# Expert weights split on GpSimd beside the choice of tokens: two low parts leave VectorE's search rounds

## What is computed

```python
def expert_choice_ffn(h, w_router, w_gate, w_up, w_down):
    B, N, D = h.shape
    cap = EC_CAPACITY_FACTOR * N // N_EXPERTS          # 256
    aff = jax.nn.softmax((h @ w_router).astype(jnp.float32), axis=-1)
    g, idx = lax.top_k(jnp.swapaxes(aff, 1, 2), cap)
    xs = jax.vmap(lambda hb, ib: hb[ib])(h, idx)
    hid = jax.nn.silu(jnp.einsum('becd,edf->becf', xs, w_gate)) * jnp.einsum('becd,edf->becf', xs, w_up)
    ys = jnp.einsum('becf,efd->becd', hid, w_down) * g[..., None].astype(h.dtype)
    return jax.vmap(lambda yb, ib: jnp.zeros((N, D), yb.dtype).at[ib.reshape(-1)].add(yb.reshape(-1, D)))(ys, idx)
```

## Time and profile before

| | us |
|---|---|
| median of 3 runs | 3572.96 |
| lowest and highest run | 3571.43, 3576.19 |
| span of the profiled execution | 3570.0 |
| PE busy in that span | 3353.1 (94%) |
| DVE busy | 1936.9 (54%) |
| ACT busy | 1366.7 (38%) |
| POOL busy | 560.6 (16%) |

### The profile page before, as it was taken

How to read it: one execution, slowest core, us unless ns; L and a number is a source line. 1 busy time by engine, 2 the same in 40 slices (tenths; PEclk the granted TensorE clock), 3 DMA queues, 4 the chain that set the end, 5 groups by cost and what they waited for, 6 DMA issues and landing times. The chain is left out here.

```text
span 3570.0 us, 75034 instructions
## 1 busy us (share of the span) xinstructions
PE 3353.1 (94%) x31456; PEld 2882.7 (81%) x31456; DVE 1936.9 (54%) x3309; ACT 1366.7 (38%) x1927; POOL 560.6 (16%) x792
## 2 busy tenths in 40 slices
PE   7999999999799998989999989929999999999997
PEld 5788888787577877878888878829999999999997
DVE  4666667666544655652122146575655565556553
ACT  5445454444256664320000013314444444444442
POOL 3455555555000000000000000000000100010001
PEclk9999999999899999999999999959999999999999
DMA  4221212211234434421111144335666666666662
GB/s 142 55 82 56 84 54 62 82 50 38 82 119 142 142 107 142 135 65 40 48 29 46 48 143 154 135 127 182 205 207 211 200 204 208 211 199 202 210 209 74
DMA packets 361076, 439.96 MB, mean 123 GB/s; under 512 B 15093, under 2 KB 300053, under 8 KB 359957
## 3 DMA queue, kind: packets, MB, share of 16 engines
q1 hardware_dynamic: 351640, 403.19, 34.5%
q0 software_dynamic: 9216, 33.56, 4.0%
HBM read 369.58 MB, written 67.13 MB: 122 GB/s over the span
## 5 line engine op out<-in xcount | busy, mean ns | idle before, releaser
L2620 PE MATMUL bank<-ex_x_hi,ex_w_lo 128*128 128x256 f32 x2048 | 581.7, 284 | 3.6 <-DVE ex_x_lo L2809 3.6
L2621 PE MATMUL bank<-ex_x_lo,ex_w_hi 128*128 128x256 f32 x2048 | 580.4, 283 | 0.0
L2622 PE MATMUL bank<-ex_x_hi,ex_w_hi 128*128 128x256 f32 x2048 | 580.2, 283 | 0.0
L2616 DVE TENSOR_TENSOR ex_w_lo<-ex_w_loaded,ex_w_hi 128x2048 fp32r<-128x2048 f32 x190 | 429.5, 2289 | 239.9 <-ACT ex_w_hi L2612 235.5
L2612 ACT ACTIVATE ex_w_hi<-ex_w_loaded 128x2048 fp32r<-128x2048 f32 x192 | 359.7, 1905 | 226.6 <-PE bank L2622 183.9
L2620 PEld LDWEIGHTS bank<-ex_x_hi,ex_w_lo 128*128 128x128 f32 x2048 | 393.8, 192 | 4.6 <-issue 4.0
L2621 PEld LDWEIGHTS bank<-ex_x_lo,ex_w_hi 128*128 128x128 f32 x2048 | 393.9, 192 | 0.6
L2622 PEld LDWEIGHTS bank<-ex_x_hi,ex_w_hi 128*128 128x128 f32 x2048 | 393.9, 192 | 0.0
L2688 POOL CAST ex_idx<-moe_idx_all 128x2 uint32 (+1 forms) x16 | 3.0, 186 | 1802.2 <-POOLq L79 1487.0
L264 PE MATMUL bank<-columns_columns_hi,weights_weights_lo 128*128 128x512 f32 x544 | 226.8, 417 | 9.4 <-DVE columns_columns_lo L848 4.4
L266 PE MATMUL bank<-columns_columns_hi,weights_weights_hi 128*128 128x512 f32 x544 | 214.1, 394 | 0.0
(11 more groups left out here) (458 smaller groups left out, 8266.0 us busy)
## 6 DMA issues: line engine op xcount, KB each, us to landing
ex_w_loaded<-in_wg SPq DMA_DIRECT2D x64, 1024.0 KB, 5.4
ex_w_loaded<-in_wu SPq DMA_DIRECT2D x64, 1024.0 KB, 6.4
ex_w_loaded<-in_wd SPq DMA_DIRECT2D x64, 1024.0 KB, 5.1
plain_weights<-in_w_in SPq DMA_DIRECT2D x70, 512.0 KB, 4.6
gl_ada_tile<-in_ada_w SPq DMA_DIRECT2D x48, 512.0 KB, 4.2
plain_columns<-hT_dram SPq DMA_DIRECT2D x14, 1024.0 KB, 7.4
sc_w_loaded<-in_sc_w_in SPq DMA_DIRECT2D x23, 512.0 KB, 6.5
plain_columns<-in_x SPq DMA_DIRECT2D x16, 512.0 KB, 5.8
```

Source lines behind the costliest of these rows:

```text
L2616: nc.vector.tensor_tensor(w_lo[c % SPLIT][:], raw[:, c % LOADED, :], w_hi[c % SPLIT][:].bitcast(F32), ALU.subtract).then_inc(s["lo"], 1)
L2620: nc.tensor.matmul(psum, ll, rh, start=first, stop=False)
L2621: nc.tensor.matmul(psum, lh, rl, start=False, stop=False)
L2622: return nc.tensor.matmul(psum, lh, rh, start=False, stop=last)
```

## The change

GpSimd gets a body in the block of `choose`: it waits for the high part of chunk 0 and subtracts it from the loaded chunk in one instruction of 128 x 2048, then the same for chunk 1, and counts up `lo` after each. VectorE's twelve pieces are taken out of the rounds, with their waits.

```diff
@@ choose
             def _(act):
                 beside.scalar(act)
 
+            @block.gpsimd
+            def _(pool):
+                beside.pool(pool)
+
             @block.vector
             def _(dve):
                 go = Line(dve, s["chain_v"])
@@ choose, search
                         parts(n + r)
-                        beside.vector(dve, n + r)
                         go.settle()
                         dve.wait_ge(s["summed"], n + r + 1)
@@ experts, class Beside
-            def vector(self, dve, r):
-
-
-                c, piece = divmod(r - 3, 6)
-                if 0 <= c < 2:
-                    of = slice(piece * 352, min(piece * 352 + 352, W))
-                    if piece == 0:
-                        dve.wait_ge(s["hi"], c + 1)
-                    ins = nc.vector.tensor_tensor(w_lo[c][:, of], raw[:, c, of], w_hi[c][:, of].bitcast(F32), ALU.subtract)
-                    if piece == 5:
-                        ins.then_inc(s["lo"], 1)
+            def pool(self, pool):
+
+                for c in range(2):
+                    pool.wait_ge(s["hi"], c + 1)
+                    nc.gpsimd.tensor_tensor(w_lo[c][:], raw[:, c, :], w_hi[c][:].bitcast(F32), ALU.subtract).then_inc(s["lo"], 1)
```

## The result

The changed kernel takes 3579.01 us (median of 20 runs, 3575.13 to 3583.78) against 3573.02 (20 runs, 3569.34 to 3576.19). The ratio is 1.0018, with a 95% interval of 1.0012 to 1.0025. It is slower by 6 us. The median lies inside the bound of 0.2%, the upper end of the interval beyond it.

The account below looks back on a forecast made before the run. The kernel was taken as TensorE-bound where it has work, the changed stretch as bound by a VectorE chain. Stalls of 3.1 + 3.2 less a gain of 1.1 give 5.2 us lost: 3572.96 + 5.2 = 3578.2 us, range 3570.8 to 3582.3.

Parts of the forecast that it names:

- The bound, and that a loss arrives whole: Choice of tokens: a VectorE chain sets the time; each microsecond won or lost in the rounds arrives at the end.
- The gain without the pieces, 1.1 us: Rounds 3 to 14: taking twelve pieces off VectorE wins 0.6 in rounds 3 and 4, 0.5 in eight later rounds.
- GpSimd's subtraction, 4.57 us: Each 128x2048 subtraction on GpSimd, extended from the 512 and 1024 column times; 4.9 us kept for the range.
- What is stopped, until when, and who goes next: Rounds 0 and 1: two-tensor SBUF instructions wait for GpSimd's whole instruction, then VectorE goes before GpSimd's next.
- Stall one: Round 0: `cand` (L2440) waits for the end of GpSimd's first subtraction; 3.1 us lost.
- Stall two: Round 1: `low` (L2432) waits for the end of GpSimd's second subtraction; 3.2 us lost.
- The casts pass: Round 0: the `parts` casts L2410 and L2411, slower per column than L887, aren't stopped by GpSimd.
- the rival that I gave 0.12: Round 0: casts L2410 and L2411 are stopped by GpSimd's two subtractions; 8.0 us lost, 3581.0 us; chance 0.12.
- The counts pass: Rounds: accumulating counts L2429 with one SBUF tensor aren't stopped; the rival that they are, or GpSimd keeps its turn: 0.10.
- no stall: Rival: the rounds' tiny instructions don't meet GpSimd, only the 1.1 us gain stays, 3571.9 us; chance 0.11.
- GpSimd keeps its turn: Rival: GpSimd's second subtraction starts before L2440; 6.5 us lost, 3579.5 us; chance 0.10 together with counts stopped.
- Moved loads cost nothing: SyncE's loads 4 and 5 go out about 18 and 27 us earlier and hold up nobody on the path.

Follow-up runs that it names:

- e11: Against before: GpSimd makes twelve 352-column pieces in step with the rounds, VectorE makes low parts 4 and 5 after the gathered tokens' low parts; 3568.83 us, ratio 0.9988.
- e2: Against before: pieces taken out of VectorE, GpSimd does nothing, ScalarE writes plain copies as low parts 0 and 1; 3571.58 us, ratio 0.9999.
- e7: The changed kernel with GpSimd's first subtraction waiting until round 0's casts are done; 3580.14 us, ratio 1.0021 against before.
- e1: The kernel before with GpSimd's two subtractions added and VectorE's twelve pieces kept; 3582.61 us, ratio 1.0026 against before.
- e5: The changed kernel with VectorE's small instructions of rounds 0 to 4 in accumulating one-tensor form, casts staying in round 0; 3580.26 us, ratio 1.0018 against before.
- e8: The changed kernel with round 0's casts held back until GpSimd has begun; 3580.68 us, ratio 1.0020 against before.
- e10: The kernel before plus four GpSimd fills of 128x2048 that read nothing, nothing taken away; one run, stretch 74.64 us, +2.58 against before.

## Why the prediction was right, and where it wasn't

- **The bound, and that a loss arrives whole.** Right. The distance from the last round to the first expert matmul is 27.9 us in before, in the change and in every kernel here but e11.
- **The gain without the pieces, 1.1 us.** Right: 1.19 in e2. The round trip of 0.50 read in round 8 is 0.49 to 0.50 in every round of e2 from 4 on. Round 4 gave 0.4 in place of 0.3.
- **GpSimd's subtraction, 4.57 us.** Right: 4.51 and 4.52 in e7, where nothing delays it. In the change's profile the first took 4.81; 0.3 us of it may be the second cast, which ran until 2344.83.
- **What is stopped, until when, and who goes next.** Right for the instructions with two tensors: `cand` and `low` are the ones stretched, they end 0.02 us after GpSimd's, and between GpSimd's two instructions VectorE goes first.
- **The sum, 5.2 us against 5.8.** Stall one is the mis-sized term: 3.84 in place of 3.1. GpSimd started 0.5 us later, counted from the start of the choice (8.77 us in place of 8.23), since the first chunk landed later, and took 0.24 longer. Stall two was 3.10 in place of 3.2.
- **The casts pass.** Wrong. This step read L2410's joined row of 0.87 as 0.44 for each of two, compared it with L887 per column and took the pace for a sign of another way through the engine. By line each takes 0.52 to 0.61 us, and pace was no evidence: casts are stopped (e1, e5, e8, e10). In the profile of the change they were merely issued before GpSimd started, the last of them by 0.02 us. By the times of the trace before, GpSimd would have started at 2345.43, before two of the three casts were issued, and that is the rival that I gave 0.12. In the eleven other profiles the first high part is done within 0.25 us of the time of that trace, so it deserved far more. That the profiled execution shows the two stalls that I named is luck: its first chunk landed late. The rival's price, 8.0 us, was somewhat high: 8.5 in e1 without the gain, so 7.3 with it, and 7.9 less its own hold of 0.6 in e8. So the two cases lie 1.2 to 1.5 us apart, and the forecast of the time is little off whichever of them the other runs met.
- **The counts pass, no stall, GpSimd keeps its turn.** That the counts pass was right in every trace here; the other two rivals fell with the profile of the change.
- **Moved loads cost nothing.** Right: the change's loads 4 and 5 go out 17 and 27 us earlier than before, counted from the start of the choice, and its rounds from the third on take the times of e2's, to 0.01 us, though e2's loads go out later.

## What to carry to other kernels

Work moved to an idle GpSimd is free only if VectorE's critical chain issues nothing beside it that it meets: instructions with two tensors in SBUF, casts and plain `tensor_scalar` (L887 and L943 of the prediction), however small. Look at each such instruction on the chain, and take up to the length of the whole GpSimd instruction as its price. Cut GpSimd's work into pieces that fit beside what isn't met (here the accumulating instructions, the comparison that reads PSUM among them, and waits), and start each piece by a semaphore from the chain. By the stretch, that turned a loss of 5.8 us into a gain of 1.1.

## What the runs showed of the hardware that I had not expected

- An instruction of one column is held up as readily as one of 512 (L2436, 3.25 us in place of 0.15); a broadcast operand doesn't spare it (L2443, 4.00 in place of 0.16).
- A cast holds GpSimd up as well: in e10 the second of four fills, 1.80 us by itself, took 2.90 while a cast had been waiting at its start.
- With nothing between the counts and the comparison (e5, rounds 1 to 4) the round trip over TensorE takes 0.41 us; with the small `pre` in between, 0.50. So the 0.50 that I read in round 8 isn't TensorE's alone, though VectorE stood idle for 0.28 of it; why the small instruction lengthens it isn't shown.
